# Other products between the values and the transposes of the even layer's attention

## The reference

```python
def even_layer(h, pos, norm_mix, w_in, ..., glu_w, glu_b, w_out, norm_ffn, w_gate, w_up, w_down):
    proj = rms_norm(h, norm_mix) @ w_in
    u, q, k, v = split_cols(proj, EVEN_SPLITS)          # 4 x 512 columns
    y_a = s5_mixer(u, ..., glu_w, glu_b)                # 512 columns
    y_b = moba_attention(partial_rope(heads(q), pos), partial_rope(heads(k), pos), heads(v))
    h = h + jnp.concatenate([y_a, y_b.reshape(Bsz, S, MOBA_WIDTH)], axis=-1) @ w_out
    return h + swiglu(rms_norm(h, norm_ffn), w_gate, w_up, w_down)
```

```python
    y = jax.nn.gelu(y)
    y = y * jax.nn.sigmoid(y @ glu_w.astype(f32) + glu_b.astype(f32))
```

## Time and profile before

| | us |
|---|---|
| median of 3 runs | 1488.34 |
| lowest and highest run | 1485.01, 1490.13 |
| the profiled execution | 1490.55 |
| its span, first to last instruction | 1488.6 |
| PE busy in it | 1427.8 (96%) |
| DVE busy | 706.2 (47%) |
| ACT busy | 257.2 (17%) |

### The profile page before, as it was taken

One profiled execution on the slowest core, in us unless ns is written; L12 is line 12 of the kernel. 1 busy time (PEld: TensorE's weight loads), 2 busy tenths in 40 slices (PEclk: granted clock), 3 DMA queues, 4 the chain that ended last, 5 costly groups with the idle time before them and its releaser, 6 DMA issues.

```text
span 1488.6 us, 38844 instructions
## 1 busy us (share of the span) xinstructions
PE 1427.8 (96%) x17911; PEld 1111.2 (75%) x17911; DVE 706.2 (47%) x1417; ACT 257.2 (17%) x425; POOL 30.3 (2%) x33
## 2 busy tenths in 40 slices
PE   7998999998998889999999999999999999999996
PEld 6856999998886889667667667667667667676565
DVE  5952554435489663345235235335324334343338
ACT  2334353334335212100000000000000000000001
POOL 0000000000000210000000000000000000001000
PEclk9998999999999999999999999999999999999998
DMA  9141555445330008899999999999999999999994
GB/s 313 38 170 38 206 211 176 164 155 179 127 128 1 3 3 344 335 395 409 414 398 409 414 396 410 414 386 410 413 384 412 413 389 411 413 404 409 413 379 170
DMA packets 116649, 433.79 MB, mean 291 GB/s; under 512 B 10107, under 2 KB 13285, under 8 KB 109190
## 3 DMA queue, kind: packets, MB, share of 16 engines
q1 hardware_dynamic: 112032, 420.59, 72.4%
q10 hardware_dynamic: 2982, 5.45, 1.0%
q0 software_dynamic: 1472, 5.24, 1.0%
HBM read 426.42 MB, written 4.85 MB: 290 GB/s over the span
## 4 chain that ended last, share of the span: by engine, by line
PE 89%; DVE 6%; DMA 2%; ACT 1%; issue 1%; SPq 0%; DVEq 0%; ACTq 0%
PE bank L2682 34%; PE bank L2687 22%; PE bank L2228 5%; PE bank L2230 5%; PE bank L2229 5%; PE bank L1970 3%; DMA ring<-in_moe_w_gate 2%; PE bank L2298 2%; PE bank L2216 1%; PE bank L2201 1%; PE bank L2138 1%; PE bank L2221 1%; DVE xnT L1103 1%; PE bank L2521 1%; PE bank L2519 1%
## 5 line engine op out<-in xcount | busy, mean ns | idle before, releaser
L2682 PE MATMUL bank<-ring,yT 128*32 128x384 f32 x5760 | 628.4, 488 | 4.8 <-DMA ring<-in_moe_w_gate 3.5
L2687 PE MATMUL bank<-ring,yT 128*32 128x256 f32 (+1 forms) x3264 | 628.8, 355 | 0.0
L2687 PEld LDWEIGHTS bank<-ring,yT 128*32 128x32 f32 x3264 | 356.1, 110 | 134.1 <-issue 0.7
L2682 PEld LDWEIGHTS bank<-ring,yT 128*32 128x32 f32 x5760 | 228.8, 110 | 51.5 <-issue 15.0
L2687 PE MATMUL bank<-ring,arena 128*32 128x256 f32 x1152 | 252.6, 379 | 0.0
L2682 PE MATMUL bank<-ring,arena 128*32 128x384 f32 x2304 | 252.1, 486 | 0.0
L1826 DVE STREAM_TRANSPOSE arena<-arena 32x256 f32<-32x256 f32 x288 | 188.6, 655 | 108.7 <-PE bank L2687 104.8
L1877 DVE TENSOR_TENSOR arena<-arena,bank 128x384 f32<-128x384 f32 (+1 forms) x56 | 32.1, 609 | 375.9 <-PE bank L2687 235.2
L2230 PE MATMUL bank<-arena_r,ring_r 128*128 128x256 f32 x608 | 171.7, 282 | 0.0
L2687 PEld LDWEIGHTS bank<-ring,arena 128*32 128x32 f32 x1152 | 126.5, 110 | 58.2
L2228 PE MATMUL bank<-arena_r,ring_r 128*128 128x256 f32 x528 | 148.0, 280 | 1.3 <-DVE arena_r L1356 1.3
(11 more groups left out here) (478 smaller groups left out, 1246.5 us busy)
## 6 DMA issues: line engine op xcount, KB each, us to landing
ring<-in_moe_w_gate SPq DMA_DIRECT2D x56, 2048.0 KB, 22.1
ring<-in_moe_w_up SPq DMA_DIRECT2D x56, 2048.0 KB, 22.1
ring<-in_moe_w_down SPq DMA_DIRECT2D x56, 2048.0 KB, 20.3
ring<-in_ffn_w_gate SPq DMA_DIRECT2D x5, 2048.0 KB, 7.8
ring<-in_ffn_w_up SPq DMA_DIRECT2D x5, 2048.0 KB, 7.9
ring<-in_ffn_w_down SPq DMA_DIRECT2D x5, 2048.0 KB, 8.8
ring<-in_o_w_in SPq DMA_DIRECT2D x5, 2048.0 KB, 7.7
ring<-in_e_w_in SPq DMA_DIRECT2D x4, 2048.0 KB, 16.8
```

What stands on the lines that cost most here:

```text
L2682: pe_.matmul(bank[b + i][QUAD[m], 0:FM], x(m), w[:, FB * i:FB * i + FM], start=start, stop=stop, skip_group_check=True)
L2687: last = pe_.matmul(bank[b + i][QUAD[3], o:o + n * P].rearrange("p (i n) -> p i n", i=n), x(m), side, start=start and o == 0, stop=stop, s ...
```

## The change

1. **PE, items between.** The even layer's `attention` now gets a `between`: the item that follows `("attn", u)` in the plan (`v`, `inner`, `y`, `out`) is issued between the value products of unit u-2 and the transposes of unit u-1, no longer after them.
2. **PE, last units.** In steps 7 and 8 `between` issues products of the attention half of the output projection: tiles 2 to 5 (banks 3 and 4) with k = 4 and 5, 8 products, after `o_copied` of unit 3; then k = 6, 4 products, after `o_copied` of unit 5. Ahead of step 9 come tiles 0 and 1 (bank 2) with k = 4 to 6, 6 products, after `y_added`. After the plan: the gate products first, then k = 7 of tiles 0 to 5 (6 products), then tiles 6 and 7 in full (8 products), then the S5 half as before.
3. **DVE.** `scores(u)` stands ahead of `normalise(u-1)`.
4. **ACT.** The GELU stands ahead of the last output copy (unit 7) instead of behind it.

The products are the same in number and size; only their order differs. The core of the diff:

```diff
             elif what == "attn":
+                if i == UNITS + 1:
+                    act.wait_ge(sem("y_added"), 1)
+                    act_.activation(flat(yT[:, 0:KM]), flat(yT[:, 0:KM]), ACT.Gelu_apprx_tanh).then_inc(
+                        sem("gelu_done"), 1)
                 attention(i, 0, p_even, L0["pT"], lambda w: yT[:, KM + w // NT, w % NT * P:w % NT * P + P])
-        act.wait_ge(sem("y_added"), 1)
-        act_.activation(flat(yT[:, 0:KM]), flat(yT[:, 0:KM]), ACT.Gelu_apprx_tanh).then_inc(sem("gelu_done"), 1)
...
             elif what == "attn":
-                softmax(i, 0, p_even, lambda u: C(f"causal{u % NT}"), None)
+                if i < UNITS:
+                    scores(i, 0, p_even, lambda u: C(f"causal{u % NT}"))
+                if 1 <= i <= UNITS:
+                    normalise(i - 1, 0, p_even)
...
+        def attention_half(tiles, ks):
+
+            for i in tiles:
+                loaded(5 + i // 4)
+                for k in ks:
+                    pe_.matmul(half(bank[2 + i // 2], i), view(5 + i // 4)[:, k, (i % 4) * P:(i % 4) * P + P],
+                               yT[:, k, :], start=(k == KM and i % 2 == 0), stop=False, skip_group_check=True)
+
+        def behind_values(what, i):
+
+            if what == "inner":
                 within_chunk(i)
             elif what == "y":
                 chunk_outputs(i)
+            elif what == "out":
+                turn_outputs()
...
+            elif i == UNITS - 1:
+                pe.wait_ge(sem("o_copied"), 2 * NT)
+                attention_half(range(2, 6), (KM, KM + 1))
+            elif i == UNITS:
+                pe.wait_ge(sem("o_copied"), 3 * NT)
+                attention_half(range(2, 6), (KM + 2,))
...
             elif what == "attn":
                 if i in (1, 3):
                     pe.wait_ge(sem("proj_copied"), 5 + i // 2)
+                if i == UNITS + 1:
+                    pe.wait_ge(sem("y_added"), 1)
+                    attention_half((0, 1), range(KM, KD - 1))
+                item = dict(zip(plan, plan[1:])).get(("attn", i), ("", 0))
...
-                          lambda: pe.wait_ge(sem("rope_done"), 4), p=att0)
+                          lambda: pe.wait_ge(sem("rope_done"), 4), p=att0,
+                          between=lambda: behind_values(*(item if item[0] != "attn" else ("attn", i))))
...
-        pe.wait_ge(sem("y_added"), 1)
+        gate_products()
         pe.wait_ge(sem("o_copied"), UNITS)
-        for i in range(KD):
-            if i % 4 == 0:
-                loaded(5 + i // 4)
-            if i == 4:
-                gate_products()
-            for k in range(KM, KD):
-                pe_.matmul(half(bank[2 + i // 2], i), view(5 + i // 4)[:, k, (i % 4) * P:(i % 4) * P + P],
-                           yT[:, k, :], start=(k == KM and i % 2 == 0), stop=False, skip_group_check=True)
+        attention_half(range(6), (KD - 1,))
+        attention_half((6, 7), range(KM, KD))
```

More of the change, by code:

```diff
@@ L1295, in scores @@
                 sem("nb_ready"), 1)
[L1297 to L1301, removed]
         def rope(x, pb, tmp, done):
@@ L2148, in _ @@
                 chunk_outputs(i)
+            elif what == "out":
+                turn_outputs()
+            elif what == "v":
+                if i == 0:
+                    pe.wait_ge(*step("kernel_ready"))
+                last = project_v(1, range(4 * i, 4 * i + 4))
+                if i:
+                    last.then_inc(sem("proj_done"), 1)
+            elif i == UNITS - 1:
[4 more added lines that the diff above has]
+                attention_half(range(2, 6), (KM + 2,))
+        for what, i in plan:
+            if what in S5_STEPS and what != "out":
+                S5_STEPS[what]()
             elif what == "proj":
@@ L2162, in _ @@
                 last.then_inc(sem("proj_done"), 1)
[L2163 to L2168, removed]
             elif what == "rope":
```

## The result

| | before | after |
|---|---|---|
| median, us | 1488.34 (5 runs, 1485.01 to 1490.13) | 1480.21 (5 runs, 1476.04 to 1481.53) |
| profiled execution: time, span | 1490.55, 1488.6 | 1478.22, 1476.3 |
| first scores of the even layer's attention | 88.11 | 87.62 |
| first product of the FFN | 164.10 | 153.32 |
| between these two | 75.99 | 65.70 |

The ratio is 0.9928 with a 95% interval of 0.9909 to 0.9947. Measured a second time beside other runs of the kernel before it was 0.9928 again (0.9903 to 0.9954). Of 1488 us that is 10.7 us; the stretch that the change touches is 10.29 us shorter.

The account below looks back on a forecast made before the run. PE was taken as the bound, holding 89% of the chain that ended last. Waits of 8.0 us plus half clock 3.4 gave 11.4, less 0.9 new cost: gain 10.5, median 1477.8 us, range 1474 to 1483.5.

Parts of the forecast that it names:

- Output copy: Transposes waiting for ACT to empty bank 7: six waits of 0.47 or 0.48 us, together 2.8, all gone.
- Transpose copy: Values waiting for the transpose copy, now covered only by scores: 0.06 and 0.03 us left, three times each, 0.3 new cost.
- the second rival: Transpose copy becomes the wait of every step: 3.4 us instead of 0.3, gain 7.4, time 1480.9; chance 8%.
- Unit 6: Values of unit 6, with no scores behind the transposes to cover the copy: a wait of 0.45 us in full.
- `out`: Item `out` waits for ACT's copy of `y`, now behind unit 4's transpose copy: 0.2 us, between zero and 0.6.
- DVE, GELU, GLU: Division on DVE, GELU ahead of the gate products, and S5 half's sigmoid and product: no waits; GELU margin 0.2 us.
- The clock: PE stays at 2.4 GHz through the last units, since the long waits go; 3.4 us of half-clock cost comes back.
- The first rival: Clock falls all the same near unit 6's gap, 10.2 us over dense work: costs 5.1, gain 5.4, 1482.9; chance 9%.
- The fourth rival: Clock falls in the last units and stays low up to the FFN: costs 19 us, 8.5 slower, 1496.8; chance 3%.
- The third rival: Weight transfers from 560 us on set the end and do not move with PE: time stays 1488.3; chance 6%.

Follow-up runs that it names:

- clock_filler: Kernel before plus 8 extra products with unread results in the two long waits of the last units; stretch 72.64 us against 75.99, ratio 0.9990.
- gelu_behind: Changed kernel with the GELU behind the last output copy again, as before; stretch 68.59 us against 65.70 with the change.
- step7_empty: Changed kernel with none of step 7's 8 output products there, moved to step 8 or behind the plan; stretch 69.88 us against 65.70.
- dve_only: Kernel before with only the DVE exchange, scores ahead of the division; stretch 90.00 us against 75.99, ratio 1.0089.
- items_only: Kernel before with items between values and transposes, without output products in the last units; stretch 74.17 us against 75.99, ratio 0.9979.
- step7_half: Changed kernel with only 4 of step 7's 8 output products there, the rest behind the plan; stretch 66.48 us against 65.70.
- gap_filled: Changed kernel with two of step 7's products moved between transposes and values of unit 6; stretch 65.16 us against 65.70, ratio to before 0.9949.

## Why the prediction was right

- *The sum.* 10.5 us were predicted, 10.29 came in the stretch, with the FFN's first product at 153.32 for the foretold 153.6 (the attention itself begins 0.49 earlier, at 87.62 for 88.11). The idle time fell by 7.2 us for 8.0 - 0.9 = 7.1, the busy time by 3.1 for the clock's 3.4. As the clock alone is worth 3.35 (clock_filler), about 0.3 us of busy time was added, for which the sum had nothing. The three blocks of 8, 4 and 6 output products last 3.56, 1.83 and 2.69 us from their start to the start of what follows, some 0.1 each more than the same number at 0.43, which would be the 0.3; the prediction had put the satisfied waits in front of them at nothing, at most 0.1 each. No run isolates this.
- *The median.* 1477.8 was predicted and 1480.21 measured, 2.4 us more. The first medians' difference of 8.1 and the ratio's 10.7 lie on both sides of 10.5, so how near the median came says little beside the scatter of single executions. (The 2.9 us of scatter at the low end of the range doesn't follow from the runs it names, half of whose spread is 2.6; nothing hangs on it.)
- *Output copy.* All six waits went. Right.
- *Transpose copy.* The gaps are 0.06 us for odd units (scores of unit 7 end at 115.66, values of unit 5 begin at 115.72) and 0.05 for even ones (111.91 and 111.96): 0.3 in all, as foretold. Counted from start to start each step lost 0.12 us, for the gap cuts the overlap of the groups too; but the waits that went had cut it as well. The copy started 0.03 or 0.04 us behind the modelled end of the transposes here too (114.37 + 0.66 = 115.03, and 115.06). That a matmul's end is an estimate, as the Trainium skill says (Perfetto Trace Analysis, section Tensor Engine Instruction), stays true; in this trace the estimate was good enough for covers of some hundredths, and the second rival did not come.
- *Unit 6.* 0.47 for 0.45.
- *`out`.* 0.05 us for 0.2: ACT's copy of `y` began at 111.81, 0.28 after the transpose copy ahead of it began (111.53), though that copy lasts 0.38 and the sum had 0.36; the two overlap by 0.1 in the records, which adding lengths doesn't see. The term was too large by 0.15.
- *DVE, GELU, GLU.* No waits, as foretold. The GELU's margin was 0.1 for 0.2, and gelu_behind shows that it is real: 2.9 us without the move.
- *The clock.* It stayed at 1.00. That the long waits had brought it down, which the prediction took from one trace, was then shown by clock_filler: 3.35 us for 3.4.
- *The first rival* was mis-sized. It took the low stretch to be 10.2 us wherever it falls. In step7_empty and four times in dve_only, where products without a gap lay under it, it lasted 3.4; it lasted 10.2 in before, items_only and once in dve_only, where the same three waits (0.47, 0.69 and 0.43) lie under it. That the waits make it long fits all eight, but no run tests it by itself. By the short stretch the rival's price was 1.7, not 5.1, and its time 1479.5, not 1482.9.
- *The fourth rival* let the clock stay down in one piece. No low stretch in the runs' attention lasted longer than 10.2 us, though dve_only has 23.9 in five pieces. Its sum is wrong besides: work that lasts 38 us at full clock takes 76 at half, so it costs 38 more and not 19, and its time would be some 1516, not 1496.8. That doesn't touch the forecast, since the rival was outside the range either way.
- *The third rival* fell as above: the part with the weights of the experts moves with the rest (1324.5 us before, 1323.0 and 1327.2 after).
- *Not seen:* that the exchange on DVE is worth nothing in the company of parts 1 and 2. The prediction had called it harmless by its cover (2.13 against 2.75 us), which is right; it didn't ask whether it brought anything. The chances were not affected.

## What to carry to other kernels

When two engines hand one bank to and fro, put independent work into the longer of the two handovers and let the short necessary work cover the other; then check each cover by rows, since an exchange of order that is free with the work between costs 14 us without it. Long waits on TensorE can cost more than their length, for the clock may fall with them and the next work pays (here 1.7 to 3.4 us for each fall); later products moved into such waits pay twice. The length of one wait doesn't tell: 2.47 and 0.47 us close together brought the clock down, a single 2.36 between long dense groups did not. So look at the granted clock of the stretch. Judge a change of half a percent by the stretch between two instructions that it encloses, not by medians of a few runs.

## What the runs showed of the hardware

- A gap of 2.47 us, with 0.47 more behind 0.44 us of work, brought the clock to 1.2 GHz (step7_empty); it came back after 3.4 us, with output products running. Gaps of 0.56 and 0.47 in the same place did not bring it down (step7_half).
- In dve_only the waits of 2.36 and 1.60 us left the clock at 1.00; behind the next, 1.77, it fell at 107.9 us, and then again in every step. In before, waits of 0.47 in the same steps did not bring it down.
- The eight low stretches in these attentions lasted 3.4 us (five, with products and no gap under them) or 10.2 us (three, with waits of 0.4 to 0.7 us behind the fall).
- Float32 transposes of 128x128 followed the granted clock like products: four took 0.63 us at 1.00 and 1.08 at 0.50 (before).
- Neighbouring groups of products overlap by about 0.07 us in the records; a wait cuts that too, so filling a bracket of 0.47 us gained 0.54 (gap_filled).
- The rest of the program, the same instructions in all twelve traces, took between 1321.4 and 1330.0 us in single executions.
